# Norm gain carried with the turned x, single first tiles on two queues, and the bias line built on GpSimd

## What is computed

```python
xn = _rmsnorm(x, norm_gain[0])
h = xn @ w_in                        # 2048 x 8192: q, k, v, gate
...
bias = rel_bias[_rel_bucket(k_pos[None, :] - q_pos[:, None])]
s = jnp.einsum("bqhcd,bkhcd->bhcqk", qb, k).astype(f32) + bias[None, :, None]
p = jax.nn.softmax(s, axis=-1)
a = p[:, :, 0] - lam * p[:, :, 1]    # lam from the sums of lq1*lk1 and lq2*lk2
```

## Time and profile before

| | us |
|---|---|
| median of 3 runs (851.52 to 852.56) | 851.56 |
| the profiled execution | 852.14 |
| its span in the trace | 850.4 |
| TensorE busy in the span | 842.2 |
| DVE busy | 646.2 |
| ACT busy | 449.0 |
| GpSimd busy | 220.2 |

### The profile page before, as it was taken

The page is one execution under the profiler, slowest core; times in us unless marked ns, Lnnn a source line. Parts: engine busy times, 40 slices in busy tenths (PEclk is TensorE's granted clock), DMA queues, the critical chain, the costliest instruction groups (busy, mean ns, idle before and its releaser), DMA issues.

```text
span 850.4 us, 13797 instructions
## 1 busy us (share of the span) xinstructions
PE 842.2 (99%) x5630; PEld 769.5 (90%) x5630; DVE 646.2 (76%) x1093; ACT 449.0 (53%) x586; POOL 220.2 (26%) x75
## 2 busy tenths in 40 slices
PE   9999999999999999999999999999999999999996
PEld 9998899889998899888888899999999999988885
DVE  6569784697658784698788978999999998566651
ACT  7756543546346543556544365455554556594432
POOL 0000000000000000002000008888888887680000
PEclk9999999999999999999999999999999999999999
DMA  9977556545554556534655565555555555549502
GB/s 326 395 278 252 167 190 207 175 141 198 200 194 148 166 190 208 177 120 153 232 181 186 189 207 183 175 180 199 180 177 190 191 179 185 191 151 343 196 3 99
DMA packets 99089, 163.74 MB, mean 193 GB/s; under 512 B 3504, under 2 KB 39600, under 8 KB 98520
## 3 DMA queue, kind: packets, MB, share of 16 engines
q1 hardware_dynamic: 97408, 160.50, 55.7%
q10 hardware_dynamic: 1624, 2.45, 0.8%
HBM read 160.83 MB, written 3.69 MB: 193 GB/s over the span
## 4 chain that ended last, share of the span: by engine, by line
PE 97%; SPq 1%; DMA 1%; ACT 0%; DVE 0%; issue 0%
PE ps_acc L1205 17%; PE ps_acc L1208 17%; PE ps_acc L1207 17%; PE ps_acc L1194 14%; PE ps_acc L1191 14%; PE ps_acc L1193 14%; DMA sb_w_raw<-in_attn_w_in 1%; SPq L320 0%; PE ps_a L1296 0%; PE ps_a L1295 0%; PE ps_d L1282 0%; PE ps_d L1281 0%; PE ps_a L1294 0%; PE ps_d L1280 0%; PE ps_a L1165 0%; SPq L322 0%
## 5 line engine op out<-in xcount | busy, mean ns | idle before, releaser
L432 ACT ACTIVATE sb_w_hi<-sb_w_raw 128x2048 fp32r<-128x2048 f32 x140 | 267.1, 1914 | 253.3 <-PE ps_acc L1208 171.7
L404 POOL TENSOR_TENSOR sb_w_lo<-sb_w_raw,sb_w_hi 128x2048 fp32r<-128x2048 f32 x45 | 208.5, 4637 | 435.0 <-ACT sb_w_hi L432 435.0
L777 DVE TENSOR_TENSOR sb_w_lo<-sb_w_raw,sb_w_hi 128x2048 fp32r<-128x2048 f32 x95 | 216.2, 2289 | 103.5 <-ACT sb_w_hi L432 103.1
L1205 PE MATMUL ps_acc<-sb_conv_hi,sb_w_hi 128*128 128x256 f32 x768 | 215.0, 280 | 0.0
L1208 PE MATMUL ps_acc<-sb_conv_hi,sb_w_lo 128*128 128x256 f32 x768 | 213.8, 278 | 0.0
L1207 PE MATMUL ps_acc<-sb_conv_lo,sb_w_hi 128*128 128x256 f32 x768 | 213.7, 278 | 0.0
L1007 DVE SCALAR_TENSOR_TENSOR ps_d<-sb_uT,sb_dwT,ps_d 128x256 f32<-128x256 f32 x480 | 188.9, 482 | 4.5 <-ACT ps_d L659 4.5
L1191 PE MATMUL ps_acc<-sb_w_hi,sb_act_hi 128*128 128x512 f32 x384 | 151.4, 394 | 0.0
L1193 PE MATMUL ps_acc<-sb_w_lo,sb_act_hi 128*128 128x512 f32 x384 | 151.3, 394 | 0.0
L1194 PE MATMUL ps_acc<-sb_w_hi,sb_act_lo 128*128 128x512 f32 x384 | 151.3, 394 | 0.0
L1208 PEld LDWEIGHTS ps_acc<-sb_conv_hi,sb_w_lo 128*128 128x128 f32 x768 | 144.2, 188 | 0.0
(11 more groups left out here) (169 smaller groups left out, 841.3 us busy)
## 6 DMA issues: line engine op xcount, KB each, us to landing
sb_w_raw<-in_attn_w_in SPq DMA_DIRECT2D x60, 1024.0 KB, 5.4
sb_w_raw<-in_conv_w_in SPq DMA_DIRECT2D x64, 512.0 KB, 4.5
sb_w_raw<-in_attn_w_out SPq DMA_DIRECT2D x16, 1024.0 KB, 5.0
sb_w_raw<-in_conv_w_in SPq DMA_DIRECT2D x16, 1024.0 KB, 5.2
sb_w_raw<-in_conv_w_out SPq DMA_DIRECT2D x16, 1024.0 KB, 5.0
sb_w_raw<-in_attn_w_in SPq DMA_DIRECT2D x4, 512.0 KB, 7.8
sb_xs<-in_x SPq DMA_DIRECT2D x2, 1024.0 KB, 15.6
sb_w_raw<-in_attn_w_in SPq DMA_DIRECT2D x7, 256.0 KB, 5.4
```

Of the source, the lines that this page charges most:

```text
L404: pool.tensor_tensor(w_lo[c % RING][:], w_raw[c % RING][:], w_hi[c % RING][:].bitcast(F32), ALU.subtract).then_inc(lo_ready_pool, 1)
L432: act.activation(w_hi[slot][:], w_raw[slot][:], ACT.Copy).then_inc(hi_ready, 1)
L777: dve.tensor_tensor(w_lo[slot][:], w_raw[slot][:], w_hi[slot][:].bitcast(F32), ALU.subtract).then_inc(lo_ready, 1)
L1205: pe.matmul(into, left_hi, hi[:, kt], start=(kt == 0 and f % 2 == 0), stop=False, skip_group_check=True)
```

## The change

The norm gain of the attention layer leaves `vec_all` (now 8 x 16 + 4 columns) and stands in front of the turned x, in one tensor `x_turned` of 128 x (16 + 4096) and one tile `x_in`; the first piece brings both. All 16 tiles of the head are single pieces. ACT issues only the first piece of x; SP issues the weights of tile 0 first, then x and weights of each tile in turn, and the vectors behind tile 4. The lambda product moves on DVE from the front to behind tile 8, and ACT's wait for the vectors moves behind the head. The one-hot table and the table's matmul, with the PSUM copy on ACT, go. GpSimd copies each of the 31 runs of equal bucket from the bias table (now heads x buckets, 8 partitions) into the line and zeroes the last column; ACT waits for it before it stores the line. The counts of the PSUM bank semaphores are lowered by one where later waits name them (`A_START`, `a_free`, `a_full`).

```diff
 CHUNKS = CHUNKS_CONV + NCH * PAIRS
-HEAD = [(k, k + 1) for k in range(2 * CK)] + [(k, k + 2) for k in range(2 * CK, KT, 2)]
+HEAD = [(k, k + 1) for k in range(KT)]
...
     bucket = np.where(rel > 0, nb, 0) + np.where(n < exact, n, np.minimum(far, nb - 1))
-    hot = np.zeros((BUCKETS, REL), np.float32)
-    hot[bucket, np.arange(rel.size)] = 1.0
-    return hot
+    starts = [0] + [i for i in range(1, rel.size) if bucket[i] != bucket[i - 1]]
+    return [(at, upto, int(bucket[at])) for at, upto in zip(starts, starts[1:] + [rel.size])]
 def build(nc, x, x_turned, vectors, taps, final_gain, rel_bias, attn_w_in, attn_w_out, conv_w_in,
-          conv_w_out, conv_b_out, onehot, out):
+          conv_w_out, conv_b_out, out):
     with ExitStack() as ctx:
         def sb(name, shape, dt=F32, scope=ctx):
...
         ones = sb("ones", [P, P])
-        vec_all = sb("vec_all", [P, 9 * KT + 4])
-        vecs = vec_all[:, 0:9 * KT].rearrange("p (a k) -> p a k", k=KT)
-        lam_in = vec_all[:, 9 * KT:]
+        vec_all = sb("vec_all", [P, 8 * KT + 4])
+        vecs = vec_all[:, 0:8 * KT].rearrange("p (a k) -> p a k", k=KT)
+        lam_in = vec_all[:, 8 * KT:]
         dwT = sb("dwT", [P, KT, TAPS])
         small = sb("small", [P, 64])
         grants = sb("grants", [P, 8])
-        G_IN, G_CONV, G_HEAD, DW_B, LN_G, LN_B, B_A, B_G, B_Z = range(9)
...
             with ExitStack() as start:
-                hot = sb("hot", [BUCKETS, REL], F32, start)
-                table = sb("table", [BUCKETS, HEADS], F32, start)
+                table = sb("table", [HEADS, BUCKETS], F32, start)
                 line = sb("line", [HEADS, REL], F32, start)
-                xT = sb("xT", [P, KT, SEQ], F32, start)
+                x_in = sb("x_in", [P, KT + KT * SEQ], F32, start)
+                gain_in, xT = x_in[:, 0:KT], x_in[:, KT:].rearrange("p (k s) -> p k s", s=SEQ)
...
+        def x_piece(t, p):
+
+            k0, k1 = HEAD[p]
+            return t[:, KT + k0 * SEQ if p else 0:KT + k1 * SEQ]
+
...
                 slot, rows, _ = head_piece(p)
-                sp.dma_start(xT[:, k0:k1], x_turned[:, k0:k1]).then_inc(x_landed[p], 16)
                 if p:
-                    sp.dma_start(w_raw[slot][:, rows], w_in[:, k0:k1, 0:GW]).then_inc(piece_landed(p), 16)
+                    sp.dma_start(x_piece(x_in, p), x_piece(x_turned, p)).then_inc(x_landed[p], 16)
+                sp.dma_start(w_raw[slot][:, rows], w_in[:, k0:k1, 0:GW]).then_inc(piece_landed(p), 16)
+                if p == VECS_AT:
+                    sp.dma_start(vec_all[:], vectors).then_inc(vecs_landed, 16)
             sp.dma_start(table[:], rel_bias).then_inc(table_landed, 16)
-            sp.dma_start(hot[:], onehot).then_inc(table_landed, 16)
             sp.dma_start(dwT[:], taps).then_inc(taps_landed, 16)
...
+            pool.wait_ge(table_landed, 16)
+            runs = bucket_runs()
+            for at, upto, bucket in runs:
+                pool.tensor_copy(line[:, at:upto], table[:, bucket:bucket + 1].to_broadcast([HEADS, upto - at])
+                                 ).then_inc(line_ready, 1)
+            pool.memset(line[:, runs[-1][1]:], 0.0).then_inc(line_ready, 1)
...
-            act.dma_start(vec_all[:], vectors).then_inc(vecs_landed, 16)
-            act.dma_start(w_raw[0][:, 0:1], w_in[:, 0:1, 0:GW]).then_inc(piece_landed(0), 16)
+            act.dma_start(x_piece(x_in, 0), x_piece(x_turned, 0)).then_inc(x_landed[0], 16)
             act.wait_ge(consts_ready, 1)
             act.activation(table_probe, ones[:, 0:1], ACT.Copy)
-            act.wait_ge(vecs_landed, 16)
             for p, (k0, k1) in enumerate(HEAD):
                 slot, rows, closes = head_piece(p)
                 act.wait_ge(x_landed[p], 16)
                 for kt in range(k0, k1):
-                    act.activation(act_hi[:, kt], xT[:, kt], ACT.Copy, scale=vecs[:, G_IN, kt:kt + 1]
+                    act.activation(act_hi[:, kt], xT[:, kt], ACT.Copy, scale=gain_in[:, kt:kt + 1]
                                    ).then_inc(split_hi, 1)
                 if p:
                     act.wait_ge(piece_landed(p), 16)
                     act.activation(w_hi[slot][:, rows], w_raw[slot][:, rows], ACT.Copy
                                    ).then_inc(hi_ready if closes else head_hi, 1)
+            act.wait_ge(vecs_landed, 16)
             for i in range(NCH - ST):
                 high_part(RING + i, i, 2)
             act.wait_ge(a_full, 1)
             act.activation(lam_exp, bank_a[0][:, 0:2], ACT.Exp).then_inc(a_free, 1)
-            act.wait_ge(a_full, 2)
-            act.activation(line[:], bank_a[1][0:HEADS, :], ACT.Copy).then_inc(a_free, 1)
-            act.wait_ge(a_free, 2 + 2)
+            act.wait_ge(line_ready, len(bucket_runs()) + 1)
             act.dma_start(line_dram, line[:]).then_inc(line_stored, 16)
...
-            dve.wait_ge(vecs_landed, 16)
-            dve.tensor_tensor(lam_prod, lam_in[:, 0:4:2], lam_in[:, 1:4:2], ALU.mult).then_inc(lam_prod_ready, 1)
...
+                    dve.wait_ge(vecs_landed, 16)
+                    dve.tensor_tensor(lam_prod, lam_in[:, 0:4:2], lam_in[:, 1:4:2], ALU.mult
+                                      ).then_inc(lam_prod_ready, 1)
             for i in range(NCH - 1):
                 low_part(RING + i, i)
             dve.wait_ge(ss_ready, 2)
...
-            def sums_and_line():
+            def lambda_sums():
                 free_a(0)
                 pe.wait_ge(lam_prod_ready, 1)
                 pe.matmul(bank_a[0][:, 0:2], ones[:], lam_prod, start=True, stop=True).then_inc(a_full, 1)
-                free_a(1)
-                pe.wait_ge(table_landed, 32)
-                pe.matmul(bank_a[1][0:HEADS, :], table[:], hot[:], start=True, stop=True).then_inc(a_full, 1)
...
-    features = np.concatenate([inputs[name].reshape(-1, P) for name in
-                               ("norm_gain", "attn_head_gain", "conv_dw_b", "conv_ln_g", "conv_ln_b", "conv_b_in",
+    features = np.concatenate([inputs["norm_gain"][1].reshape(KT, P)] + [inputs[name].reshape(-1, P) for name in
+                               ("attn_head_gain", "conv_dw_b", "conv_ln_g", "conv_ln_b", "conv_b_in",
                                 "attn_lq1", "attn_lk1", "attn_lq2", "attn_lk2")])
     laid_out = {
         "x": inputs["x"],
-        "x_turned": inputs["x"][0].reshape(SEQ, KT, P).transpose(2, 1, 0),
+        "x_turned": np.concatenate([inputs["norm_gain"][0].reshape(KT, P).T,
+                                    inputs["x"][0].T.reshape(KT, P, SEQ).transpose(1, 0, 2).reshape(P, KT * SEQ)], axis=1),
         "vectors": features.T,
         "taps": inputs["conv_dw"][0].reshape(TAPS, KT, P).transpose(2, 1, 0),
     }
     for name in ("final_gain", "rel_bias", "attn_w_in", "attn_w_out", "conv_w_in", "conv_w_out", "conv_b_out"):
-        laid_out[name] = inputs[name]
-    laid_out["onehot"] = bucket_onehot()
+        laid_out[name] = inputs[name].T if name == "rel_bias" else inputs[name]
```

More of the change, by code:

```diff
@@ L48 @@
 CHUNKS = CHUNKS_CONV + NCH * PAIRS
-HEAD = [(k, k + 1) for k in range(2 * CK)] + [(k, k + 2) for k in range(2 * CK, KT, 2)]
+HEAD = [(k, k + 1) for k in range(KT)]
+VECS_AT, LAM_AT = 4, 8
 WARM_UP = 9
@@ L53, with bucket_runs @@
 POOL_SEAM = CHUNKS_ATT + RING - 1
-def bucket_onehot():
+def bucket_runs():
     rel = np.arange(-(SEQ - 1), SEQ)
@@ L94, in build @@
         grants = sb("grants", [P, 8])
-        G_IN, G_CONV, G_HEAD, DW_B, LN_G, LN_B, B_A, B_G, B_Z = range(9)
+        G_CONV, G_HEAD, DW_B, LN_G, LN_B, B_A, B_G, B_Z = range(8)
         lam_prod = small[:, 4:6]
@@ L189, in build @@
         lam_prod_ready, lam_exp_ready = sem("lam_prod_ready"), sem("lam_exp_ready")
-        line_stored = sem("line_stored")
+        line_ready, line_stored = sem("line_ready"), sem("line_stored")
         windows_stored = sem("windows_stored")
@@ L237, in build @@
         G_CONV_IN = G_OUT + PAIRS
-        A_START, A_PER_PAIR = 3, 2
+        A_START, A_PER_PAIR = 2, 2
         A_CONV = A_START + A_PER_PAIR * PAIRS
@@ L557, in _ @@
                 if i == 7:
-                    act.wait_ge(a_full, 3)
+                    act.wait_ge(a_full, 2)
                     act.activation(rstd_bc, bank_a[0][:, 0:SEQ], ACT.Copy).then_inc(a_free, 1)
-                    act.wait_ge(a_free, 2 + 3)
+                    act.wait_ge(a_free, 2 + 2)
                 pair_slot(0, i)
@@ L801, in _ @@
                     dve.wait_ge(split_hi, kt + 1)
-                    dve.scalar_tensor_tensor(act_lo[:, kt], xT[:, kt], vecs[:, G_IN, kt:kt + 1],
+                    dve.scalar_tensor_tensor(act_lo[:, kt], xT[:, kt], gain_in[:, kt:kt + 1],
                                              act_hi[:, kt].bitcast(F32), ALU.mult, ALU.subtract
@@ L812, in _ @@
                                   ALU.subtract).then_inc(lo_ready if closes else head_lo, 1)
+                if p == LAM_AT:
+                    dve.wait_ge(vecs_landed, 16)
```

(12 more changed lines are left out.)

## The result

Medians of the same session: 853.09 us (852.61 to 854.35) for the changed kernel, 851.89 (851.44 to 852.56) for the one before; the ratio is 1.0016, 95% interval 1.0009 to 1.0022. So it is slower by 1.2 us (0.14%): inside the range of the prediction, and on the slow side of its 852.0. The profiled execution took 852.83 with a span of 851.0, against 852.14 and 850.4.

A forecast was written before the change was run, and what follows sets the result against it. TensorE was taken to bound the kernel, with slot 4 tied to chunk 4's landing: 25.7 - 0.17 + 0.5 + 0.25 = 26.3, plus 4.4 gives slot 4 at 30.7, +0.5 us on the 851.56 median: 852.0, range 850.9 to 853.6.

The forecast's parts named there:

- What bounds the kernel: TensorE's work end to end; at slot 4 its string and the landing of chunk 4 arrive within 0.15 us.
- The signs named for the rest: TensorE wait of 1.5 to 2.5 us at slot 4, chunk 4's high part at 26 to 26.7, one shift afterwards.
- The table's matmul and the hole at tile 8: In the head, 0.95 and 0.62 us leave TensorE's string, 1.57 together; none arrives, as slot 4 waits for chunk 4.
- The start, 0 to 0.3: First weight tile may land 0.45 us earlier, but warm-up and tile 3's landing leave 0 to 0.3 us.
- Landing of chunk 4: Fifth weight chunk, first 1 MB load of SP's loop: high part at 26.3 instead of 25.7 us, slot 4 4.4 later.
- the prediction's estimate from that page: x rows off a 256-byte boundary move 9% more on x: about 0.5 us, making the sum +0.75 instead of +0.5.
- Rival B: Chunk 4 lands after 27.5 us through rows off their boundary or a dry queue: typically 853.5 us, chance 0.12.
- The shorter vectors' tile: Addresses behind the vectors' tile shift by 64 bytes: taken as 0, with 0.2 us either way.
- GpSimd's line: Off the path: 31 runs and one fill take 4.4 us, line ready by 30 us.
- The clock: Rival: TensorE idles about 2 us before slot 4 and its clock falls, costing 2 to 3 us: 854, chance 0.03.
- ACT held up: Rival: ACT's wait for the line delays work queued behind it, up to +3 us: 854, chance 0.03.
- Whole gain: Rival: chunk 4 lands by 24.2 us and all 1.57 to 1.87 us arrives: 849.7 to 850.0, chance 0.06.

The follow-up runs named there:

- e1: Changed kernel with 64 unused bytes behind the vectors' tile, so later tiles have their old addresses: 851.59 us, ratio 0.9998 to the kernel before.
- e5: e1 with the load of the taps moved from ahead of chunk 4 to the third group of the first pair: 851.22 us, ratio 0.9988.
- e10: e1 with tiles 8 to 15 loaded and split by twos again: 851.78 us, ratio 0.9998.
- e7: Changed kernel with 128 unused bytes ahead of the weights' ring alone: 852.33 us, ratio 1.0001.
- e6: Changed kernel with 128 unused bytes ahead of the weights' ring and 64 behind the vectors: 851.16 us, ratio 0.9991.
- e3: Kernel before with 192 unused bytes behind the vectors' tile and nothing else: 853.60 us, ratio 1.0023.
- e9: Kernel before with 128 unused bytes behind the vectors' tile and nothing else: 842.16 us, ratio 0.9875.

## Why the prediction came out as it did

*What bounds the kernel*: right. TensorE end to end, with slot 4 tied to chunk 4's landing by a constant 4.39 us (4.4 computed). The signs named for the rest were missed: the wait is 0.5 us where 1.5 to 2.5 was said, chunk 4's high part starts at 25.19 where 26 to 26.7 was said, and the shift behind slot 4 isn't one amount but grows and changes sign.

*The table's matmul and the hole at tile 8, 1.57 off TensorE's string, none of it arriving*: right in kind. From tile 1 to the end of slot 3 TensorE needs 1.9 us less in e1 than in before, where 1.57 was computed. With the string shorter, slot 4 waits for the low part and starts 0.15 us behind it, as computed (0.14). But the hole at tile 8 was read from one trace, and three others of the old head lack it. At equal addresses the whole change is worth 0.3 us.

*The start, 0 to 0.3*: not refuted, though the one trace of the change says otherwise (tile 1 at 7.13, was 6.91). Over all traces TensorE's first real matmul starts at 5.41 with the old head (5) and at 4.96 with the new one (9), and tile 1 at 7.03 and 6.87, that is 0.16 earlier, though within the scatter. What hides most of it is the slow stretch shown above, in which matmuls start 0.21 us apart: it ends at about 6.4 in the changed kernel and in e1, near the end of the warm-up in e5 and e10, so that tile 1 starts anywhere from 6.60 to 7.26 with one and the same head. The prediction had no such term. The turned tile, too, is later than the vectors were (ACT begins at 4.36, was 3.76). All this is hidden by the wait for chunk 4 like the rest.

*Landing of chunk 4, +0.6 (eight small loads +0.5, rows off their boundary +0.25, one-hot table -0.17)*: not borne out. By the profile -0.53, over all runs -0.1, by e10 0.06 between doubles and singles, where the scatter leaves about 0.7 either way for the second of these. The rate of a stretch was taken as a price of its row length; in the changed kernel four of the five stretches from 7 to 17 us, all with single tiles, moved 373 to 389 GB/s and one 368, where the doubles had 380:

```profile
9.00:11.00 2.00, 2.00 (x19) 2.00 (x19) 1.82 (x5) 1.81 (x4) 0.00 (x0) 1.00 1.06 389
...
13.00:15.00 2.00, 2.00 (x19) 2.00 (x18) 2.00 (x6) 1.98 (x5) 0.00 (x0) 1.00 1.07 376
15.00:17.00 2.00, 2.00 (x19) 2.00 (x19) 2.00 (x5) 1.97 (x5) 0.00 (x0) 1.00 1.06 373
```

The Trainium skill's rule (DMA: Bandwidth & Descriptors, How a descriptor splits into AXI transactions) says that a row which begins off a 256-byte boundary also fetches the bytes before it. No cost of it shows in the landings here, but the prediction's estimate from that page, 0.5 us, is within their scatter, so no run here decides it. Rival B wanted a landing after 27.5; the latest in any trace is 26.40 (e7).

*The shorter vectors' tile: 0, with 0.2 either way*: this is the step that failed. It costs 1.5 us (e1), more than the whole forecast, and is the reason why the kernel is slower at all. The prediction said that no row gave it a price, which was true, and then took a price near nothing: the bound should have been left open, since it touches 5376 matmuls that are the path.

So 852.0 was near 853.1 by luck, by two errors that partly cancel: -0.3 from the head where +0.5 was forecast, and +1.5 from addresses where 0 was. Even the direction was right for a reason that the prediction didn't have.

*GpSimd's line*: estimated 4.4 us, ready by 30. It took 5.70 and was ready at 26.5; 31 copies are 0.18 each. ACT never waited for it: its store is issued at 27.81.

```profile
20.78 5.70 POOL L409 COPY sb_line<-sb_table 8x165 f32<-8x165 f32 x31 [18.99 <-DMA sb_table<-in_rel_bias]
```

*The clock* (C) and *ACT held up* (D): neither appears; the granted clock stays 1.00 through waits of 0.5 to 1.7 us before slot 4. *Whole gain* (A): the condition, a landing by 24.2, was reached in no run with the taps ahead of it.

## What to carry to other kernels

When one engine is busy for the whole span, an edit that changes the size of any tile is an edit of every address behind it: compare the distance from start to start of its commonest instruction before and after, and repeat the change with the old addresses, before anything is credited to the edit's purpose. It is worth trying a few unused bytes between weights and activations as a parameter of its own; here 128 bytes gave 1.2%, more than the restructuring of the head could. The best value is no rule: the order of the distances was found by trying them, and within one distance the pace still changed. And where two strings meet within 0.15 us, shortening one shows only how far away the other is.

## What the runs showed of the hardware

The pace of float32r matmuls depends on where the two operands lie relative to each other. With weights and activations 0, 64, 128 and 192 bytes apart modulo 256 it is on average 120.0, 117.8, 119.7 and 114.5 ns for 256 columns and 227.0, 233.4, 232.5 and 232.8 ns for 512 (attention layer). In the 256-column form the weights are the operand that is loaded and the activations stream past, in the 512-column form it is the reverse. e6 and e7 moved both by 128 bytes and kept the pace but for e6's stretch at 113.3, and e3 (distance 0 by another 256 bytes) has that of the changed kernel. Weights were tried at two places only (0 and 128 modulo 256), and a gap moves every tile behind it, so that it is these two operands and no other pair of tiles is argued: they are all that the matmuls of the projections read from SBUF. Contention with other engines or the DMA is unlikely, since in before the 256-column pace is 117.8 ns with a DMA share of 0.64 (110 to 140 us) as in the head, where the share is over 1.00. What in the engine or the memory does it was not measured.

The averages hide that the pace has levels. At distances 64 and 192 the 256-column matmuls go at 117.8 or at 113.3 ns, for tens of us at a time, and what the distance changes is how often. At distance 64 it is 117.8 but for parts of the convolution (about 607 to 629, 681 to 709 and from 727 us on, in before and in e1 alike) and short stretches of the head in e5, e6 and e10. At distance 192 (e9) it is 113.3 over most of the attention layer and 117.8 again from about 492 to 570, 622 to 650 and 673 to 702 us. At distance 0 there is one level, 120.0. What switches between the levels stays open, and so does e7's 0.8 us.
